# Column-sum items of the modulation product cut in half, in six buffers, and a scratch fill issued later

## The reference

```
cond = jax.nn.silu(c)
for i in range(DEPTH):
    mod = cond @ ada_w[i] + ada_b[i]                      # ada_w[i]: 1024 x 6144
    sh1, sc1, g1, sh2, sc2, g2 = jnp.split(mod[:, None, :], 6, axis=-1)
    h = rms_norm(x, norm1_g[i]) * (1.0 + sc1) + sh1
    y = diff_attention(h, ...) if i % 2 == 0 else stick_breaking_attention(h, ...)
    x = x + g1 * y
    h = rms_norm(x, norm2_g[i]) * (1.0 + sc2) + sh2
    x = x + g2 * hierarchical_moe(h, ...)
```

## Time and profile before

| | |
|---|---|
| Median of three runs | 1846.84 us (1846.0 to 1852.7) |
| Profiled execution, its own time | 1846.84 us |
| Its span | 1845.0 us |
| TensorE busy | 1684.1 us, 91% of the span |
| VectorE, ScalarE, GpSimd busy | 490.1, 444.2, 158.4 us |
| Read from HBM, written | 578.87 MB, 21.32 MB |
| Mean granted TensorE clock | 0.972 |

### The profile page before, as it was taken

The page is one execution under the profiler, slowest core; times in us unless marked ns, Lnnn a source line. Parts: engine busy times, 40 slices in busy tenths (PEclk is TensorE's granted clock), DMA queues, the critical chain, the costliest instruction groups (busy, mean ns, idle before and its releaser), DMA issues.

```text
span 1845.0 us, 18530 instructions
## 1 busy us (share of the span) xinstructions
PE 1684.1 (91%) x7537; PEld 859.2 (47%) x7537; DVE 490.1 (27%) x935; ACT 444.2 (24%) x939; POOL 158.4 (9%) x236
## 2 busy tenths in 40 slices
PE   6896999888889879999999999999998999989988
PEld 4643543333333334845464344444443356565564
DVE  1357221000000103244241002221220123553362
ACT  2015211111111102015231013333331034343351
POOL 0212010000000010123000010000001000100000
PEclk9999999999999999999989999999998999999999
DMA  9989779999999999987369989999999963413310
GB/s 359 347 337 397 296 277 409 422 419 420 422 421 421 421 413 396 383 338 258 115 244 410 347 323 397 395 405 420 420 419 410 368 231 107 145 50 117 137 46 23
DMA packets 122752, 585.12 MB, mean 317 GB/s; under 512 B 11936, under 2 KB 16872, under 8 KB 99008
## 3 DMA queue, kind: packets, MB, share of 16 engines
q1 hardware_dynamic: 101008, 489.59, 66.3%
q0 software_dynamic: 21536, 88.72, 13.1%
q10 hardware_dynamic: 112, 5.51, 0.8%
HBM read 578.87 MB, written 21.32 MB: 325 GB/s over the span
## 4 chain that ended last, share of the span: by engine, by line
PE 60%; DMA 25%; DVE 6%; ACT 3%; issue 3%; SPq 3%; ACTq 0%; DVEq 0%; POOL 0%
PE psum L2204 57%; DMA ring<-in_expert_w_up 19%; DMA work<-in_ada_w 3%; SPq L1433 1%; PE psum L699 1%; DMA ring<-in_expert_w_gate 1%; SPq L1402 1%; DMA work<-in_ctx 1%; DMA ring<-in_ada_w 1%; DMA work<-in_w_mod 1%; PE psum L2508 1%; DVE small L1057 1%; PE psum L1198 1%; DVE work L1882 1%; DVE work L2099 0%
## 5 line engine op out<-in xcount | busy, mean ns | idle before, releaser
L2204 PE MATMUL psum<-ring,work 128*64 128x512 f32 (+5 forms) x4272 | 1095.4, 575 | 66.8 <-DMA ring<-in_expert_w_up 53.9
L2204 PEld LDWEIGHTS psum<-ring,work 128*64 128x64 f32 (+2 forms) x4272 | 424.3, 152 | 664.5 <-issue 635.0
L2204 PE MATMUL psum<-work 128*128 128x192 f32 (+9 forms) x1048 | 218.2, 371 | 8.1 <-DVE work L2032 2.6
L2204 PEld LDWEIGHTS psum<-work 128*128 128x128 f32 (+3 forms) x1048 | 144.9, 188 | 105.2 <-issue 81.6
L2099 DVE TENSOR_TENSOR work<-work,psum 128x256 f32<-128x256 f32 x64 | 27.0, 421 | 593.2 <-ACT work L1802 593.2
L1802 ACT ACTIVATE work<-psum 128x256 f32<-128x256 f32 x64 | 24.5, 383 | 607.7 <-PE psum L2204 607.7
L2204 PE MATMUL psum<-work,ring 128*128 128x256 f32 x704 | 158.8, 384 | 3.2 <-DMA ring<-in_diff_w_in 1.1
L2204 PEld LDWEIGHTS psum<-work,ring 128*128 128x128 f32 x704 | 133.4, 192 | 29.1 <-issue 8.1
L1669 ACT ACTIVATE work<-psum 128x256 f32<-128x256 f32 (+5 forms) x184 | 79.7, 443 | 224.7 <-PE psum L2508 76.0
L1561 POOL DMA_INDIRECT expert_rows<-work,targets x56 | 55.1, 984 | 806.6 <-DVE work L2125 806.6
L2125 DVE TENSOR_TENSOR work<-psum,rows 128x512 f32<-128x512 f32 x64 | 44.3, 692 | 255.8 <-PE psum L2204 255.7
(11 more groups left out here) (295 smaller groups left out, 956.6 us busy)
## 6 DMA issues: line engine op xcount, KB each, us to landing
ring<-in_expert_w_gate SPq DMA_DIRECT2D x60, 2048.0 KB, 16.5
ring<-in_expert_w_up SPq DMA_DIRECT2D x60, 2048.0 KB, 17.4
ring<-in_expert_w_down SPq DMA_DIRECT2D x57, 2048.0 KB, 14.4
work<-in_ada_w POOLq DMA_DIRECT2D x40, 1024.0 KB, 8.0
ring<-in_w_in SPq DMA_DIRECT2D x12, 2048.0 KB, 10.1
work<-in_w_mod POOLq DMA_DIRECT2D x16, 1024.0 KB, 6.8
ring<-in_sb_w_in SPq DMA_DIRECT2D x6, 2048.0 KB, 24.7
ring<-in_w_out SPq DMA_DIRECT2D x6, 2048.0 KB, 8.0
```

The lines of the kernel that those rows point to most:

```text
L2204: return T.matmul(out_, lhsT, rhs, start=start, stop=stop, skip_group_check=True)
```

## The change

Each item of a summed group becomes two parts of 1024 columns, 0.5 MB each. A group has 16 parts: first eight for its first 1024 columns (half 0), then eight for its second (half 1). The three buffers of 2048 columns are used as six of 1024. Parts are numbered on, two for each item, so that group 1 has parts 0 to 15 and group 2 parts 16 to 31; group 5 has parts 64 to 79. A part's load waits for the part six before it: for the sum to have gone one step beyond it, or for TensorE's product where that part is the last of a half. VectorE makes 16 steps of 1024 columns for a group and counts them in `ada_step`. TensorE makes two products for a group, two matmuls each: in layer 0 behind blocks 4, 6, 8 and 10, in layer 1 behind blocks 4, 6, 8 and 11 (before: 6 and 11 in both).

Groups that TensorE multiplies itself keep items of 2048 columns, in pairs of the small buffers.

The fill of `expert_rows` is issued when the first half of the first residual is there (`x_half`), ahead of the square of `x`, where it was issued at once after the turned attention output. Four pairs of semaphores are merged (`x_in` with `rows_set` as `x_rows`, `lam_in` with `first_bias`, `lam_exp` with `s_ln` as `log_exp`, `ada_sum` into `ada_step`).

```diff
+    ada_half = ada_in.rearrange("p i (a n) -> p (i a) n", a=2)
...
+    def used_by(g):
+
+        return sum(2 if j in SUMMED else KT for j in range(1, g + 1))
+
+    def steps_by(part):
+
+        g = group_of(part // 2)
+        return 2 * KT * SUMMED.index(g) + part - 2 * KT * (g - 1) + 1
...
             if l == 0 and n == 4:
-                sp.wait_ge(sem("ada_used"), 5)
+                sp.wait_ge(sem("ada_step"), 10)
             if l == 0 and n == 6:
-                sp.wait_ge(sem("ada_used"), KT * 2 - 3)
+                sp.wait_ge(sem("ada_step"), 2 * (KT * 2 - 3))
...
+        def half_free(part):
+
+            g = group_of(part // 2)
+            if g not in SUMMED:
+                pool.wait_ge(sem("ada_used"), used_by(g - 1) + part // 2 % KT + 1)
+            elif part % KT == KT - 1:
+                pool.wait_ge(sem("ada_used"), used_by(g - 1) + part // KT % 2 + 1)
+            else:
+                pool.wait_ge(sem("ada_step"), steps_by(part + 1))
+
         def ada_load(i):
 
             g, t = group_of(i), i % KT
+            if g in SUMMED:
+                for part in (2 * i, 2 * i + 1):
+                    if part >= 6:
+                        half_free(part - 6)
+                    half, t = part // KT % 2, part % KT
+                    which, c = GROUPS[g][2 * half]
+                    src = a["ada_w"][which][:, c * 512:(c + 2) * 512].rearrange("(p t) n -> p t n", t=KT)[:, t, :]
+                    pool.dma_start(ada_half[:, part % 6, :], src).then_inc(sem(f"ada_in{part % 6}"), 16)
+                return
             if i >= 3:
-                before = group_of(i - 3)
-                if before in SUMMED and (i - 3) % KT == KT - 2:
-                    pool.wait_ge(sem("ada_sum"), SUMMED.index(before) + 1)
-                else:
-                    pool.wait_ge(sem("ada_used"), i - 1 if before in SUMMED and (i - 3) % KT < KT - 2 else i - 2)
+                half_free(2 * i - 6)
+                half_free(2 * i - 5)
...
                 take_oT(l)
-                finite = a["expert_w_down"][0, 0:3].rearrange("e f d -> (e f) d")[0:TAIL * LIST, :]
-                act.dma_start(expert_rows, finite).then_inc(sem("rows_set"), 16)
             else:
                 stick_act(act, link, copy)
+            if l == 0:
+                act.wait_ge(sem("x_half"), 1)
+                finite = a["expert_w_down"][0, 0:3].rearrange("e f d -> (e f) d")[0:TAIL * LIST, :]
+                act.dma_start(expert_rows, finite).then_inc(sem("x_rows"), 16)
             square_norm(2 * l + 1)
...
-            for t in range(KT):
-                i = KT * (g - 1) + t
-                now, before = ada_in[:, i % 3, :], ada_in[:, (i - 1) % 3, :]
-                dve.wait_ge(sem(f"ada_in{i % 3}"), in_count(i))
-                if t:
-                    dve.wait_ge(sem("ada_used"), i)
-                    ins = V.scalar_tensor_tensor(now, now, cond[:, 0, t:t + 1], before, ALU.mult, ALU.add)
+            for t in range(2 * KT):
+                part = 2 * KT * (g - 1) + t
+                now, before, factor = ada_half[:, part % 6, :], ada_half[:, (part - 1) % 6, :], cond[:, 0, t % KT:t % KT + 1]
+                dve.wait_ge(sem(f"ada_in{part % 6}"), in_count(part))
+                if t % KT:
+                    dve.wait_ge(sem("ada_step"), steps_by(part - 1))
+                    ins = V.scalar_tensor_tensor(now, now, factor, before, ALU.mult, ALU.add)
...
             if g in SUMMED:
-                pe.wait_ge(sem("ada_sum"), SUMMED.index(g) + 1)
+                half = i % KT
+                last = 2 * KT * (g - 1) + KT * half + KT - 1
+                pe.wait_ge(sem("ada_step"), steps_by(last))
                 pe.wait_ge(*((sem("ada_row"), g - 1) if g > 1 else (sem("first_line"), 3)))
-                for k in range(4):
-                    ins = mm(bank[7][32 * k:32 * k + 1, :], C["ones"][:, 0:1], ada_in[:, i % 3, 512 * k:512 * (k + 1)], True, True)
+                for k in range(2):
+                    r = 64 * half + 32 * k
+                    ins = mm(bank[7][r:r + 1, :], C["ones"][:, 0:1], ada_half[:, last % 6, 512 * k:512 * (k + 1)], True, True)
                 ins.then_inc(sem("ada_used"), 1)
...
-        QKV_ITEMS = [[[KT * SUMMED[2 * l + (i == 11)] - 1] if i in (6, 11) else [] for i in range(12)] for l in range(2)]
+        SUM_BEHIND = (4, 6, 8, 10), (4, 6, 8, 11)
+        QKV_ITEMS = [[[KT * (SUMMED[2 * l + j // 2] - 1) + j % 2 for j in range(4) if SUM_BEHIND[l][j] == i] for i in range(12)]
+                     for l in range(2)]
```

More of the change, by code:

```diff
@@ L202, in group_of, with in_count @@
         return 1 + i // KT
-    def in_count(i):
-        return 16 * sum(len(runs(group_of(j))) for j in range(i % 3, i + 1, 3))
+    def in_count(part):
+        loads_of = lambda j: 1 if group_of(j // 2) in SUMMED else len(runs(group_of(j // 2))) * (j % 2 == 0)
+        return 16 * sum(loads_of(j) for j in range(part % 6, part + 1, 6))
+    def used_by(g):
[3 more added lines that the diff above has]
+        return 2 * KT * SUMMED.index(g) + part - 2 * KT * (g - 1) + 1
     def line_count(g):
@@ L656, in stream_rms @@
             act.wait_ge(sem("y_in"), 16)
-            act.wait_ge(sem("ada_used"), KT * LAST1)
+            act.wait_ge(sem("ada_used"), used_by(LAST1))
         elif p == 1:
@@ L1479, in _ @@
             if l == 0:
-                sp.wait_ge(sem("ada_used"), KT * 3)
+                sp.wait_ge(sem("ada_used"), used_by(3))
             for e in range(NX):
@@ L1874, in ada_sum @@
         def ada_sum(g):
-            for t in range(KT):
-                i = KT * (g - 1) + t
-                now, before = ada_in[:, i % 3, :], ada_in[:, (i - 1) % 3, :]
-                dve.wait_ge(sem(f"ada_in{i % 3}"), in_count(i))
-                if t:
-                    dve.wait_ge(sem("ada_used"), i)
-                    ins = V.scalar_tensor_tensor(now, now, cond[:, 0, t:t + 1], before, ALU.mult, ALU.add)
-                else:
-                    ins = V.tensor_scalar(now, now, cond[:, 0, t:t + 1], None, ALU.mult)
-                ins.then_inc(sem("ada_used" if t < KT - 1 else "ada_sum"), 1)
+            for t in range(2 * KT):
[5 more added lines that the diff above has]
+                    ins = V.scalar_tensor_tensor(now, now, factor, before, ALU.mult, ALU.add)
+                else:
+                    ins = V.tensor_scalar(now, now, factor, None, ALU.mult)
+                ins.then_inc(sem("ada_step"), 1)
         def first_norm():
```

28 lines of the change are left out of this document (14 added, 14 removed).

## The result

The changed kernel takes 1855.43 us (median of 10 executions, 1851.35 to 1863.33), the kernel before 1848.48 us on the same chip (10 executions, 1845.01 to 1852.7). The ratio is 1.0044, 95% interval 1.0031 to 1.0056. The forecast was 1846.3, range 1840 to 1852. The profiled execution took 1853.11, its span is 1851.3 us against 1845.0.

A forecast was written before the change was run, and what follows sets the result against it. The prediction took TensorE as the bound (60% of the chain that ended last, DMA 25%). Head -4.3, entry -0.6, copy +0.7 and layer 1 +3.7 gave -0.5 us: 1846.84 to 1846.3 us, range 1840 to 1852.

The forecast's parts named there:

- Head, -4.3: Layer 0's QKV stage: block 11 ends at 124.6 instead of 129.45; with 0.5 us of clock loss, 4.3 us gained.
- The 7.15 us are gone: Layer 0, behind block 6: part 15 is summed at 83.3, so TensorE's wait of 7.15 us disappears.
- The change doesn't do what it says: Rival: ada_w gets half the DMA rate, block 6's wait grows to 10 us, total 1853.6; chance 0.02.
- The step on the weights: Layer 0's QKV weights: weight 5 lands at 103, between 97.5 and 107.2, so block 9 waits from 98.4.
- the rival with equal turns: Rival: queues alternate equally, weight 5 lands at 107.2, TensorE idles 8.8 us before block 9; total 1852.2, chance 0.10.
- 4 to 1: DMA split between ada_w and QKV weights before the change, 324 to 81 GB/s, taken as queues alternating row by row.
- Entry, -0.6: Entry of layer 0's attention: group 2's addition and the lambda vector lie earlier, leaving some 2.9 us; 0.6 us gained.
- A microsecond won or lost in the head is therefore worth about one at the end: Whole program: a shift early in the program reaches the end about one for one, because TensorE releases later stages.
- Products, 0.52 us "by half of 1.04": TensorE's products: two of 8 matmuls become four of 4, each taking 0.52 us, half of 1.04.
- Layer 1, +3.7: Layer 1's product behind block 6 waits 0 to 6 us for part 79, behind router loads; 3.7 us lost.
- Copy, +0.7: The later fill of `expert_rows` ends at 217 to 219 and delays expert loads beside item 31; 0.7 us lost.
- my rival, which priced it at 5.3: Rival: the copy ends at 225 and item 31's load starts 5 us late; total 1851, chance 0.05.

The follow-up runs named there:

- e9: The kernel before with lambda vectors moved behind item 9, layer 0's router rows behind item 30, layer 1's behind item 57; ratio 1.0092.
- e17: The kernel before with lambda vectors behind item 9 and layer 0's router rows issued on SyncE's queue; 1846.3 us, ratio 0.9991.
- e2: The kernel before with only the copy (fill of `expert_rows`) issued late, behind `x_half`; ratio 1.0020.
- e5: The kernel before with a dummy product of two 512-column matmuls of a constant added behind blocks 4 and 8 of each layer; ratio 1.0010.
- e4: The changed kernel with each product made as four matmuls of 256 columns into rows 0, 32, 64 and 96; ratio 1.0058.
- e16: The changed kernel with the copy early, products of four 256-column matmuls, lambda vectors behind item 9, layer 0's router rows behind item 18; ratio 1.0029.
- e3: The changed kernel with the copy (fill of `expert_rows`) issued at its old, early place; ratio 1.0009 to the kernel before.
- the three pairs above: Kernels with parts against whole items, copy early, small loads in one place within each pair; medians 4.5, 4.4 and 5.6 us over.

## Why the prediction was wrong

Of the four terms of -0.5 us, the profile shows: head and entry -1.4 instead of -4.9, copy +2.0 instead of +0.7, layer 1 +2.2 instead of +3.7, and +3.7 in the attention of layer 0, which the sum put at nothing.

- **Head, -4.3.** "The 7.15 us are gone" is the first step that failed. Block 6 still waited 4.34 us, and the end of block 11 came 0.8 us earlier (121.54 + 7.13 = 128.7 against 129.45). The spacing of 1.94 us was right within 0.1 (2.04); 6.6 us for the small loads was short by 3 (9.6). Part 15 was summed at 87.6 and not at 83.3. Of the rivals "The change doesn't do what it says", with a chance of 0.02, comes nearest. The step on the weights failed too, unseen. Weight 5 landed at 105.8 and 107.5, by the rival with equal turns and not in the middle. No wait of 4 us stood before block 9 in the first profile, but that is luck: one wait covered the other. From 44 to 60 the two queues did take equal turns (packets, MB; q0 GpSimd's, q1 SyncE's):

```profile
q0 software_dynamic: 1130, 3.78, 69.5%
q1 hardware_dynamic: 1124, 2.27, 37.3%
```

  They did not in 76 to 88, where q0 had 657 packets and q1 1179, though parts were issued and not yet landed all through it. Nor did the kernel before keep to 4 to 1 over a whole stretch: from 44 to 60 it moved 3.42 MB on q0 and 3.03 on q1. My 324 to 81 GB/s were those of two items alone.
- **Entry, -0.6.** Measured: -1.4 at the attention's start less -0.8 at block 11 is -0.6.
- **"A microsecond won or lost in the head is therefore worth about one at the end".** In after it did not come out: of 1.4 us won nothing was left at 183 us. Whether the rule is wrong stays open. In e9 and e17 4 to 5 us passed through; in e2 and e5, whose attention is that of before, the same stretch lost 2.9 and 1.4 us. So chance in one execution is worth as much as the term itself, and only 0.8 to 2.3 of the 3.7 us in after are more than those two lost. The granted clock goes with it. From 155 to 183 it was 0.88 in before, 0.76 in after, 0.82 in e2 and e5, 0.94 in e17:

```profile
155.00:183.00 28.00, 18.21 (x112) 9.10 (x112) 19.31 (x53) 14.87 (x73) 4.43 (x8) 0.88 1.01 418
```
```profile
155.00:183.00 28.00, 20.61 (x113) 9.82 (x112) 18.77 (x51) 13.74 (x69) 4.36 (x9) 0.76 1.01 411
```

  (first before, then after; columns as in the earlier trace rows). TensorE was busy 20.6 of 28 us instead of 18.2, for about the same number of instructions. I had also made the sum against one profile with a favourable attention: its 1846.84 us is 1.6 below the median of ten.
- **Products, 0.52 us "by half of 1.04".** The second step that failed, shown by e4 and e5: the price goes by the length of one matmul and not by their number, 1.03 us for two of 512 columns, 1.04 for four, 0.61 for four of 256. The Trainium skill ("TensorE: Matmul & The Clock Gate", part on packing small matmuls) says that outputs in different groups of 32 partitions run side by side; the rows agree, and the earlier trace rows already showed it: in blocks of 512 columns 16 rows take 7.02 us, 0.44 each, by which the product's 8 rows would have taken 3.5 us if one ran after the other, and not 1.04.
- **Layer 1, +3.7.** The wait of 3.7 us behind the router loads did not come (0 us in after). Part 79 was issued at 778.6 and summed 8.5 us later, 1.6 us before TensorE wanted it. That is near the 7.2 us that I had without contention, and I took the upper end. 2.2 us came from the two more products, which the term did not contain: that a loss came at all is luck. The feared wait is real, though: with products only 0.4 us shorter it appeared one product later, 4.15 us in e4, 4.05 in e16.
- **Copy, +0.7.** The third step that failed, and by the ratios the dearest. The mechanism (item 31's load has no cover) was right, the size was not: 2.0 us at item 31 in the profile, and 3.7 us (1.8 to 5.5) by the ratio of e2. I chose a landing at 217 to 219; it was 225.6, as in my rival, which priced it at 5.3.
- **Which term makes the result.** By the ratios the change costs 0.0044 x 1848 = 8.1 us (5.7 to 10.3). The late copy alone costs 3.7 (e2), all of the change but the copy 1.7 (e3), together 5.4, just under the interval's lower end. With the 4.4 to 5.6 us that parts cost in the three pairs above they would make the whole. Whether e3 is low by chance, or the late copy costs more beside the parts, stays open. So does why the median of e17 gains 1 us where its profile shows 3.5, and how much of the loss in the attention is chance.

## What to carry to other kernels

Before splitting a transfer to shorten a wait, look at what shares its queue: here nine tiny loads made the wait, and moving them removed it with nothing split, whereas the split added four products. Here the price of a small product was set by the length of one matmul, since its matmuls go to different row groups; so split in columns within the product and not into more products. A wait removed is not yet time won: with block 6's wait gone another stood behind block 11 or among the items of the attention, and none of the moves here is shown to beat the kernel before. Move a small load only to a place where nobody waits behind it and its own reader is far off. And compare two profiles of one kernel before you price a difference of 2 us between two kernels.

## What the runs showed of the hardware that was not expected

- Four fp32 matmuls of 256 columns into rows 0, 32, 64 and 96 take 0.61 us together, two of 512 columns 1.03, four of 512 columns 1.04.
- Four router loads on GpSimd's queue are issued in 0.91, 0.89, 0.56 and 0.55 us in before (the earlier trace rows has two of layer 1's). On SyncE's queue the same four hold it for 26.6 us in e17:

```profile
109.72 9.76 SPq L1484 DMA_DIRECT2D work<-in_router_group_w  x1
119.52 3.62 SPq L1484 DMA_DIRECT2D work<-in_router_expert_w  x1
123.18 12.69 SPq L1484 DMA_DIRECT2D work<-in_router_group_b  x1
135.91 0.43 SPq L1484 DMA_DIRECT2D work<-in_router_expert_b  x1
```

  No wait came of it there: SyncE's next issue was that of an expert's gate weight at 153.76.
- The copy from HBM to HBM goes in packets of 57 KB (5.51 MB in 96 of them, above), and the expert weights issued at 216.28 and 216.66 moved none of theirs before 222.
- A 0.5 MB part issued just ahead of a 2 MB weight on another queue lands in 4.7 us, one issued just behind it in 9.8 (after and e4, layer 1).
